# Two attentions of a 256-token, one-core transformer kernel, with the output of each head computed transposed and the softmax sums spread by TensorE

## What is computed

```python
# first attention ("at1"): 16 heads of 64, causal, output gated
s = einsum('qd,kd->qk', q, k) * 64 ** -0.5;  s = where(k_pos <= q_pos, s, NEG)
o = softmax(s) @ v;  x = x + (o * silu(gate)) @ w_out_b
# second attention ("at3"): 8 heads, 128 + 64 (rope) wide, values 128
s = (einsum('qd,kd->qk', q_nope, k_nope) + einsum('qd,kd->qk', q_rope, k_rope)) * 192 ** -0.5
s = where(k_pos <= q_pos, s, -inf);  o = softmax(s) @ v;  y = o @ w_out
```

## Time and profile before

| what | value |
|---|---|
| median of 3 runs | 1164.64 us (1161.25 to 1164.98) |
| the profiled execution's own time | 1164.23 us |
| its span, first to last instruction | 1162.4 us |
| mean granted TensorE clock over the span | 0.981 |
| PE busy | 1085.8 us (93%) |
| DVE busy | 743.5 us (64%) |
| ACT busy | 495.9 us (43%) |
| chain that ended last, by engine | PE 76%, DVE 15%, ACT 3%, issue 2%, DMA 2% |

### The profile page before, as it was taken

How to read it: one execution, slowest core, us unless ns; L and a number is a source line. 1 busy time by engine, 2 the same in 40 slices (tenths; PEclk the granted TensorE clock), 3 DMA queues, 4 the chain that set the end, 5 groups by cost and what they waited for, 6 DMA issues and landing times.

```text
span 1162.4 us, 19633 instructions
## 1 busy us (share of the span) xinstructions
PE 1085.8 (93%) x8492; PEld 888.6 (76%) x8492; DVE 743.5 (64%) x1153; ACT 495.9 (43%) x770; POOL 33.7 (3%) x31
## 2 busy tenths in 40 slices
PE   5999979897999997999899999999899899999997
PEld 5884579895768776697657889999657677998995
DVE  6761967747569948666467677667437656554544
ACT  2422222133454467355254555354333555554442
POOL 0000005300000010000000000000000000000000
PEclk9999989999999999999899999999999999999999
DMA  9763200522257450363434567766743545474620
GB/s 388 275 247 130 88 2 3 220 76 75 94 196 269 165 217 2 140 232 136 181 130 164 227 251 294 289 276 226 281 145 145 217 145 178 184 264 171 217 74 36
DMA packets 15078, 204.88 MB, mean 176 GB/s; under 512 B 1800, under 2 KB 1800, under 8 KB 2832
## 3 DMA queue, kind: packets, MB, share of 16 engines
q1 hardware_dynamic: 14544, 202.55, 46.2%
q10 hardware_dynamic: 448, 1.08, 0.2%
HBM read 202.57 MB, written 1.05 MB: 175 GB/s over the span
## 4 chain that ended last, share of the span: by engine, by line
PE 76%; DVE 15%; ACT 3%; issue 2%; DMA 2%; SPq 0%; DVEq 0%; ACTq 0%
PE bank L432 15%; PE bank L434 15%; PE bank L433 15%; PE bank L391 5%; PE bank L700 5%; PE bank L490 5%; DVE slot_parts L1749 2%; PE bank L547 2%; DMA ring<-in_stream 1%; PE bank L503 1%; PE bank L517 1%; PE bank L610 1%; DVE arena L1877 1%; PE bank L682 1%; DVE small L1723 1%
## 5 line engine op out<-in xcount | busy, mean ns | idle before, releaser
L432 PE MATMUL bank<-page_parts 128*128 128x512 f32 (+1 forms) x1104 | 378.3, 343 | 4.9 <-DVE page_parts L1782 2.5
L1749 DVE TENSOR_TENSOR slot_parts<-ring,page_parts 128x2048 fp32r<-128x2048 f32 x104 | 236.9, 2288 | 120.6 <-ACT page_parts L1194 120.3
L1194 ACT ACTIVATE page_parts<-ring 128x2048 fp32r<-128x2048 f32 x104 | 197.7, 1910 | 139.8 <-PE bank L434 88.0
L432 PEld LDWEIGHTS bank<-page_parts 128*128 128x128 f32 x1104 | 210.4, 191 | 29.7 <-issue 4.3
L433 PE MATMUL bank<-slot_parts,page_parts 128*128 128x512 f32 x576 | 225.6, 392 | 0.0
L434 PE MATMUL bank<-page_parts 128*128 128x512 f32 x576 | 225.5, 391 | 0.0
L1251 ACT ACTIVATE arena<-bank 128x512 f32<-128x512 f32 (+1 forms) x142 | 78.7, 572 | 211.4 <-PE bank L490 66.6
L433 PE MATMUL bank<-page_parts 128*128 128x256 f32 x528 | 149.4, 283 | 0.0
L434 PE MATMUL bank<-page_parts,slot_parts 128*128 128x256 f32 x528 | 149.4, 283 | 0.0
L434 PEld LDWEIGHTS bank<-page_parts 128*128 128x128 f32 x576 | 108.9, 189 | 23.2
L433 PEld LDWEIGHTS bank<-slot_parts,page_parts 128*128 128x128 f32 x576 | 109.2, 190 | 21.6
(11 more groups left out here) (285 smaller groups left out, 1230.6 us busy)
## 6 DMA issues: line engine op xcount, KB each, us to landing
ring<-in_stream SPq DMA_DIRECT2D x95, 2048.0 KB, 8.3
arena<-in_x SPq DMA_DIRECT2D x2, 512.0 KB, 4.4
gn<-in_gn ACTq DMA_DIRECT2D x2, 512.0 KB, 13.0
out<-arena SPq DMA_DIRECT2D x2, 512.0 KB, 2.6
cc<-in_consts SPq DMA_DIRECT2D x1, 898.0 KB, 6.6
pc<-in_params SPq DMA_DIRECT2D x1, 287.5 KB, 6.9
gn<-in_head_sel ACTq DMA_DIRECT2D x1, 32.0 KB
pos_i<-in_positions ACTq DMA_DIRECT2D x1, 1.0 KB, 4.0
```

The costliest lines, as they stand in the source:

```text
L432: mm(out, a[0], b[0], start=start, stop=False)
L1194: act(unit_parts(n)[0], unit_values(n)[1], ACT.Copy).then_inc(ac.step("w_hi"), 1)
L1749: tt(unit_parts(n)[1], lo, hi, ALU.subtract).then_inc(dv.step("w_lo"), 1)
```

## The change

- Both attentions compute pv with the values as weights and the transposed probabilities streamed, so the output is feature-major (heads' features on partitions, tokens along the bank). In at1 two heads (64 features each) fill the two column groups of the array; this is one group of two heads, and in at3 one head is a group. A bank holds one group: 256 columns of output and 256 of inverse sums. The outputs use banks 6 and 7, scores and transposes now six banks.
- The inverse sums (`rs`, by `invert` on DVE, L2086) are spread over the partitions by PE: a matmul with the sum column broadcast as weights against the identity (L581 of the changed kernel). PE waits for `at1_r` or `at3_r` before it.
- Scores are computed for two heads at once. The q and k rows of the two heads lie on partitions 0 to 63 and 64 to 127, and the matmuls of the two alternate between the row groups of the array. The zeroed copies are gone, and so are four of the six POOL fills.
- Mask and maximum are one `tensor_tensor_reduce` for each token block (L2096, "ISA" in the listings), each with a read-out of its accumulator.
- After each group DVE multiplies output, inverse sums and (at1) the gate into the transposed page, and splits every second group there (`split_pair`). The 16 transposes after each attention, the late gate products and `split_h` at this place are gone. In at3 ACT copies the output out of the bank first (`On`).
- The gate g1 of at1 is now made feature-major, by `split_T` in place of `split_tok`, in two panels.

```diff
             def attention(name, heads, dv, scores, V):
-                per = 512 // (TB * dv)
+                group = P // dv
...
+                def pv(g):
+                    b = claim((name, "O", g), 6 + g % 2)
+                    hs = range(g * group, (g + 1) * group)
+                    for h in hs:
+                        pe.wait_ge(*evacuated((name, "PT", h)))
+
+                    for kb, n, start, stop in ((0, 0, True, True), (0, 1, True, False), (1, 2, False, True)):
+                        for h in hs:
+                            rows = slice(h % group * dv, (h % group + 1) * dv)
+                            mm(b[rows, (n > 0) * P:(n > 0) * P + P], V[:, kb, h * dv:(h + 1) * dv], PTs[:, h % 4, n * P:(n + 1) * P],
+                               start=start, stop=stop)
+                    pe.wait_ge(sem(name + "_r"), g + 1)
+                    for tb in range(TB):
+                        for h in hs:
+                            rows = slice(h % group * dv, (h % group + 1) * dv)
+                            ins = mm(b[rows, T + tb * P:T + (tb + 1) * P], rs[:, h, tb:tb + 1].to_broadcast([P, dv]), ident,
+                                     start=True, stop=True)
+                    ins.then_inc(filled((name, "O", g)), 1)
...
                 for h in range(heads + 2):
-                    if h < heads:
-                        score(h)
+                    if h < heads and h % 2 == 0:
+                        scores(h, [claim((name, "S", h + hp)) for hp in range(2)])
                     if 1 <= h <= heads:
                         turn_p(h - 1)
-                    if h >= 2:
-                        pv(h - 2)
+                    if h > group and (h - 1) % group == 0:
+                        pv((h - 1) // group - 1)
...
-                    tt(Ss[:, h % 2, :], bank((name, "S", h))[:, 0:3 * P], con("causal"), ALU.add).then_inc(dv.frees((name, "S", h)), 1)
+                    for tb, cs in ((0, slice(0, P)), (1, slice(P, 3 * P))):
+                        V.tensor_tensor_reduce(Ss[:, h % 2, cs], bank((name, "S", h))[:, cs], con("causal")[:, cs], 1.0, 3.0 * NEG,
+                                               ALU.add, ALU.max, accum_out=mx[:, 2 * (h % 2) + tb:2 * (h % 2) + tb + 1]).then_inc(
+                            dv.frees((name, "S", h)) if tb else dv.step(), 1)
                     dve.wait_ge(*dv.last)
-                    V.tensor_reduce(mx[:, 0:1], Ss[:, h % 2, 0:P], AX.X, ALU.max).then_inc(dv.step(), 1)
-                    V.tensor_reduce(mx[:, 1:2], Ss[:, h % 2, P:3 * P], AX.X, ALU.max).then_inc(dv.step(), 1)
...
+                    ts(nmax[:, h, :], mx[:, 2 * (h % 2):2 * (h % 2) + 2], -scale, None, ALU.mult).then_inc(dv.step(name + "_max"), 1)
+                    invert(h - 1)
+                    if (done + 1) * group <= h - 3:
+                        finish(done)
...
+            def gated_pair(j):
...
+                tt(On[:, j % 2, :], bank(p)[:, 0:T], G1T[:, j, :], ALU.mult).then_inc(dv.step(), 1)
+                dve.wait_ge(*dv.last)
+                tt(O1T[:, j, :], On[:, j % 2, :], bank(p)[:, T:2 * T], ALU.mult).then_inc(dv.frees(p), 1)
+                if j % 2:
+                    split_pair("o1T", j // 2, O1_PAGES)
...
-            transposes("o1T", O1, ready=lambda i: (sem("o1"), 1 + i // 3))
...
-            transposes("o3T", O3, ready=lambda i: evacuated(("at3", "O", i)))
```

More of the change, by code:

```diff
@@ L1428, in _, with attention @@
             ada_turned()
-            def attention(name, heads, dv, scale, early):
-                for h in range(heads + 1):
+            def attention(name, heads, dv, scale, early, kept=None):
+                group = P // dv
+                for h in range(heads + (3 if kept else 1)):
                     if h < heads:
@@ L1472, in _ @@
                         plain("k1T", K1T)
-                        pairs("q1T", Q1T_OF)
+                        plain("q1T", Q1T)
                 if name == "q1":
@@ L1620, in _ @@
             ins.then_inc(ac.frees("ckvT"), 1)
-            pair(KRT_OF, "krT", T)
+            copy(KRT, "krT", T)
             for half in range(2):
@@ L1633, in _ @@
             u = unit_of["wo_d", 0]
-            attention("at3", MH, DV, MLA_SCALE, {n // 2 + 1: [(u + n // 4, n % 4 - 1), (u + n // 4, n % 4)] for n in range(1, 8, 2)})
-            page_used.update({p: finished(("at3", "O", 3)) for p in (3, 4, 14)})
+            attention("at3", MH, DV, MLA_SCALE, {n // 2 + 1: [(u + n // 4, n % 4 - 1), (u + n // 4, n % 4)] for n in range(1, 8, 2)}, On)
+            page_used.update({p: finished(("at3", "O", MH - 1)) for p in (3, 4, 14)})
             split(unit_of["wo_d", 0] + AHEAD)
-            plain("o3T", O3T)
             ada_columns()
@@ L1770, in split_output, with split_pair @@
                 split(unit_of[name, 1] + 1)
+            def split_pair(name, i, pages):
+                js = slice(2 * i, 2 * i + 2)
+                value = page(pages[0], KT)[:, js, :]
+                hi, lo = (a[:, js, :] for a in split_parts(pages))
+                dve.wait_ge(*dv.last)
+                V.tensor_copy(hi, value).then_inc(dv.step(), 1)
+                dve.wait_ge(*dv.last)
+                tt(lo, value, hi.bitcast(F32), ALU.subtract).then_inc(dv.step(name + "_split"), 1)
             def split_h(name, *buffers):
@@ L2325, in _, with divided_head @@
             u = unit_of["wo_d", 0]
-            attention("at3", MH, DV, MLA_SCALE, O3, quarters_from(4, u, 2), lambda: ada(1))
-            split_output("wo_d", "o3T", O3_PAGES)
+            def divided_head(h):
+                p = ("at3", "O", h)
+                dve.wait_ge(sem("at3_o"), h + 1)
+                tt(O3T[:, h, :], On[:, h % 2, :], bank(p)[:, T:2 * T], ALU.mult).then_inc(dv.frees(p), 1)
+                if h % 2:
+                    split_pair("o3T", h // 2, O3_PAGES)
+            attention("at3", MH, DV, MLA_SCALE, divided_head, quarters_from(4, u, 2), lambda: ada(1))
+            split(unit_of["wo_d", 1] + 1)
             modulation(22, 26, (4,))
```

150 lines of the change are left out of this document (68 added, 82 removed).

## The result

The changed kernel takes 1167.22 us (median, 1163.71 to 1171.17), the kernel before on the same chip 1162.69 us (1157.31 to 1166.08). The ratio is 1.0039, with an interval of 1.0028 to 1.0051: 4.5 us slower. The profiled execution of the changed kernel took 1167.09 us with a span of 1165.3 us at a mean granted clock of 0.973; before they were 1164.23, 1162.4 and 0.981.

A forecast was written before the change was run, and what follows sets the result against it. No engine was taken to bound either attention throughout, only the path of hand-overs, with DVE bounding at3's last four heads. Terms 0.9 - 0.9 + 0.5 + 2.0 = +2.5 us on 1164.23 gave 1166.7 us, range 1160 to 1174.

The forecast's parts named there:

- g1, +0.9: Gate g1: 256 streamed columns a matmul cost 0.6 us in the second panel and about 0.3 in the first.
- The pieces of a pair: at1: the steps of one pair of heads, layout changes at 0.20 us each included, sum to 4.98 us against 4.61.
- rival with a nearly hidden change: Both attentions: layout change costs 0.05 us, not 0.20, and extra slow spells don't come; 1162 or 1160 us; chance 0.25.
- at1, -0.9: First attention: walk over the heads +1.4 us, tail after the last value product -2.3 us, together -0.9 us.
- the waits on DVE (0.6): at1: DVE late in three of six pairs, with weight and pair splits ahead of the next mask; 0.6 us.
- the slow start (0.5): at1: 0.5 us added for the slow clock that opens the stage in both kernels.
- at3, +0.5: Second attention: head 4's mask +1.9 us later, DVE's work then +0.8, wo_d starting at 939.0 against 938.47.
- then DVE bounds: at3 from head 4's mask on: DVE sets the time, +0.8 us on 14.32, over 90% busy.
- The clock, +2.0: Both attentions: longer PE idle spells bring one more slow spell in each stage, +2.0 us together.
- clock in every pair: at1: idle spells of 1.8 us halve the clock in each pair; 1173 us, up to 1175; chance 0.13.
- the signs: Expected trace readings, among them at1 from first scores to wo_b 43 to 44.5 us and clock under 0.96 in both stages.
- a single slow spell in each attention: at1 and at3: one extra spell at half clock per stage, about 1 us for a pair's PE work.

The follow-up runs named there:

- e11: Kernel before with joined mask and maximum, each head's scores one head earlier, and g1 by 256 streamed token columns; 1147.67 us, ratio 0.9867.
- e5_filled: Changed kernel with six unread identity matmuls ahead of each even head's transposes in at1; 1159.37 us, ratio 0.9976 to the kernel before.
- e2_at3_only: Kernel before with only the second attention (at3) as in the changed kernel; 1162.17 us, ratio 1.0010.
- e7_unfused: Changed kernel with mask and the two maxima as three separate instructions again; 1180.98 us, ratio 1.0153 to the kernel before.
- e3: Kernel before with only mask and maximum joined into fused instructions; 1149.77 us, ratio 0.9909.
- e4: Kernel before with only gate g1 changed, to matmuls of 256 streamed columns in place of 512; 1165.14 us, ratio 1.0037.
- e8: Kernel before with joined mask and maximum and each head's scores issued one head earlier; 1144.92 us, ratio 0.9852.
- e12: Kernel before with only each head's scores issued one head earlier, mask and maxima unjoined; 1153.22 us, ratio 0.9922.
- e1: Changed kernel with the second attention (at3) as before, so only at1 and g1 changed; 1167.37 us, ratio 1.0049 to the kernel before.
- e6: Changed kernel with the next pair's scores issued ahead of the value product and spread; 1154.67 us, ratio 0.9945 to the kernel before.
- e9: Changed kernel with the next pair's scores early and four unread identity products a pair in at1; 1152.07 us, ratio 0.9911 to the kernel before.
- e10: Changed kernel without the spread of inverse sums and its wait from each attention's third group on; 1168.31 us, ratio 1.0063 to the kernel before.

## Why the prediction came out as it did

The forecast was +2.5 us on the profiled execution and 1166.7 us; measured were 1167.22 us and +4.5. The total is close in part by luck, because errors of both signs met: the clock cost more than forecast, at1 and the stages behind it less. By its own steps:

- **g1, +0.9.** Right for the second panel: 11.68 against 11.01 us. The 0.3 of the first wasn't measured. That the same edit costs 4.3 us alone and 1.8 in e11 was not foreseen.
- **The pieces of a pair.** Right within 0.12 us each: scores to mask 0.21 us (predicted 0.33), mask to exponential 0.94 (predicted 1.03), hand-over to the transposes 1.13 (1.13), transposes and layout change 0.45 (0.56), values 0.71 (0.65), spread 0.54 (0.43), layout change and scores 0.85 (0.85). The pair is 4.83 us at full clock, for 4.98. The pairs overlap, and a layout change costs 0.09 us (transposes, 0.36 without it) to 0.20 (scores, 0.65 without it), where the prediction took 0.20 from the earlier trace rows. The 0.05 of the rival with a nearly hidden change is under both. What the Trainium skill's "TensorEngine Tiling (Array Packing)", Key Properties, says of a drain at a change of mode fits these rows, which show the price and not its mechanism.
- **at1, -0.9.** Mis-sized. The prediction's parts make 43.1 us for the stage (41.7 + 0.5 + 0.9); with the clock at 1.00 in e5_filled it is 40.34. From one pair's scores to the next there are 4.77 us, so that the six pairs put in at 29.9 are 28.6; the first pair is 3.5 (put in at 3.9); the waits on DVE (0.6) and the slow start (0.5) never came. Against 43.83 before this is -3.5, of which some 1.3 us is the slow spell that the kernel before has there (3.4 us at 0.37). The term should have been about -2.2, if the unread products cost nothing themselves.
- **at3, +0.5.** Nearly right, step by step, at full clock. In e2_at3_only head 4's mask comes 914.46 - 901.08 = 13.38 us after the first scores, as put in (4.9 + 6.0 + 2.48; against the kernel before that is +2.0, where the text rounds it to +1.9). The step "then DVE bounds" held: from head 4's mask to the end of head 7's work DVE is busy 14.22 of 15.19 us in the changed kernel (94%, predicted over 90), and the length is the predicted one (14.32 + 0.8). At full clock the stage is 32.64 us there, +1.1 against 31.55, and the run measures the part at 1.0010, 1.2 us. In the changed kernel's own profile it is 33.94, since a spell at half clock (3.4 us, clock 0.95 over the stage) makes its second pair longer. What the prediction put too late are the waits on DVE, which it had for the last two value products only. The value product of head h waits for DVE's product of head h - 2 (L2347), which stands on DVE's queue behind the mask of head h + 2. Such a wait comes five times, from head 2's value product to head 6's, 0.95 to 1.80 us each:

```profile
922.36 0.29 DVE L2096 CUSTOM_DVE_ANT_0 arena<-bank,cc 128x128 f32<-128x128 f32 x1 [3.08 <-PE bank L1118]
...
923.19 0.40 DVE L2347 TENSOR_TENSOR arena<-arena,bank 128x256 f32<-128x256 f32 x1
...
923.64 0.94 PE L575 MATMUL bank<-arena 128*128 128x128 f32 x6 [0.95 <-DVE arena L2347]
...
926.65 0.94 PE L575 MATMUL bank<-arena 128*128 128x128 f32 x6 [1.30 <-DVE arena L2347]
...
930.13 0.55 PE L563 MATMUL bank<-cc,arena 128*128 128x128 f32 x3
```

  The pair ahead of this took 922.15 - 916.03 = 6.12 us, as predicted (6.1), this one 7.98. Of these DVE is busy 7.15, and its one longer idle time is 0.69 us before the next even head's mask, which waits for PE's scores.
- **The clock, +2.0.** This is the term that was mis-sized most, and the rival "clock in every pair" described what happens in at1: a half clock for 30.6 of 51 us in the profiled execution, against 3.4 in the kernel before, and 50.92 us from the first scores to wo_b, where the signs had 43 to 44.5. Over the runs the changed kernel has 13 to 17 us more at half clock than the kernel before, at 0.37 us some 5 to 6 us in place of 2.0. The spells themselves were foreseen: PE's weight loads stood idle 1.33 us in the kernel before and 1.75 in the changed one, for a predicted 1.8 (PE itself 0.95 and 1.38). What failed is the step from there to a single slow spell in each attention. The rival's chance was kept at 0.13 because spells of 1.33 us had left at1 at 0.96; spells of 1.75, one a pair with a busy PE between them, went with a half clock for most of the stage, and filling them removed it. A spell's length alone doesn't decide: in e7_unfused the same spells are 0.87 us longer, and at1's clock is 0.78 and not 0.70. The busy share of the stage doesn't either: 35.84 of 54.62 us in e7 went with 0.78, 37.61 of 50.92 with 0.70. What exactly decides stays open. The Trainium skill's "TensorE: Matmul & The Clock Gate", HAM oscillation, tells of a clock that falls in the waits between bursts of matmuls, with waits for DMA as its first case; here the waits were for ACT.
- **A gain that the prediction lacks.** It had PE full outside the attentions, so that what an attention gains or loses moves everything behind it one for one. That was not so. In the kernel before PE waits 1.17 us at 555.38 for a copy by DVE, which stands behind two splits of a stream; a spell of 6.83 us at half clock begins during that wait (timeline, then windows, of the kernel before):

```profile
551.90 4.49 DVE L1749 TENSOR_TENSOR slot_parts<-ring,page_parts 128x2048 fp32r<-128x2048 f32 x2 [1.35 <-ACT page_parts L1194]
...
556.31 0.18 DVE L2216 COPY small<-bank 128x32 f32<-128x32 f32 x1
...
556.55 1.22 PE L1045 MATMUL bank<-arena 128*128 128x256 f32 x2 [1.17 <-DVE small L2216]
```

```profile
555.56:562.39 6.83, 5.83 (x15) 4.69 (x16) 1.80 (x5) 0.52 (x1) 0.00 (x0) 0.50 0.99 425
```

  In the changed kernel the same product doesn't wait for it:

```profile
561.05 0.70 PE L1046 MATMUL bank<-arena 128*128 128x256 f32 x2
...
562.05 0.18 DVE L2232 COPY small<-bank 128x32 f32<-128x32 f32 x1
```

  The wait stands in the traces of all kernels with at1 in its old layout (e2, e3, e4, e8, e11, e12) and of none with the new (e1, e5, e6, e7, e9, e10). In these six traces and that of the kernel before a spell of 3.4 or 6.8 us at half clock lies at this place, and in none of the seven with the new layout. The attention's claims of banks differ (six in rotation in place of five, and other output banks), so that the product lands in another bank; that this is the cause was argued from the releaser and not tested. The wait and the spell behind it can make up most of the 5.2 us between the attentions in the profiled pair (1.17 and, for 6.83 us at 0.37 to 0.45 each, 2.5 to 3.1).

The terms as the traces and runs have them make 0.9 (g1, of which 0.6 is measured) - 2.2 (at1 at full clock) + 1.1 (at3 at full clock) + 5 to 6 (clock) - 1.2 (the missing wait) = +3.6 to +4.6 us, against 4.5 measured. This is an estimate, since several of them rest on the 0.37. The clock term is taken over whole executions, so the missing spell behind 555 us is already in it.

## What to carry to other kernels

Shorten the hand-overs before the work: where no engine is full, an order that issues the next scores one step earlier (-9 us) and a joined mask (-11 us) gained. Pairing the heads on PE lost: it put the value product and spread of a whole pair in front of the next scores (11 us by the order alone) and left PE idle for longer at a stretch, which went with a half clock (7 us by the filler). Where PE idles on the path, look at the clock of the stage first: a filler of a few unread products was worth 7 us there, and the run that took real work out of PE was no faster. And read the other stages too: a shifted rotation of buffers may take out or put in a wait 90 us later.

## What the hardware showed

- Unread products in the waits raised the clock of at1 from 0.70 to 1.00 and took the stage from 50.92 to 40.34 us; the effect on whole executions was 7.3 us.
- In e7_unfused half and full clock alternate within each pair of at1 (a pair is 6.80 us; 0.50 in 441.13:444.55, 1.00 in 444.55:447.96, 0.50 in 447.96:451.37), while the changed kernel stays at half for 23.89 us. Both idle in every pair, the first for longer (2.25 us against 1.38): the longer idle spells went with the shorter slow ones.
- Between the attentions, where PE is nearly full, e9_early_filled (none at half clock) takes 435.4 us and the kernel before (10.2 at half) 441.2, which also has the wait of 1.17: (5.8 - 1.2) / 10.2 = 0.45 us for each. The changed kernel (3.4 at half) takes 436.0, which gives 0.2. So these traces don't tell whether a microsecond at half clock costs more there than the 0.37 of the attentions.
- Mask with maximum of 256 columns from PSUM takes 0.42 us and 0.08 for the read-out of the maximum, and the same form from SBUF the same; one starts 0.46 us before what follows its read-out in both. No cost of the source shows.
